# Attention values as the stationary operand, two outputs of a head side by side in TensorE's columns, turned back afterwards

## What is computed

```python
def attend(q, k, v, map_w):
    s = jnp.einsum('bqhmd,bkhmd->bhmqk', q, k).astype(jnp.float32)
    p = jax.nn.softmax(s, axis=-1)
    w = jnp.einsum('bhmqk,mh->bhqk', p, map_w.astype(jnp.float32))
    return jnp.einsum('bhqk,bkhd->bqhd', w.astype(v.dtype), v)
```

## Time and profile before

| what | value |
|---|---|
| profiled execution's own time | 4513.33 us |
| span of its instructions | 4511.4 us |
| mean granted TensorE clock | 0.92 |
| TensorE matmul busy | 3802.8 us (84%) |
| VectorE busy | 1758.7 us (39%) |
| ScalarE busy | 1679.3 us (37%) |
| L893, products with the values | 2624 records, 350.7 us busy |
| L882, transposes of probabilities | 1312 records, 225.2 us busy |
| L867, scores | 800 records |

### The profile page before, as it was taken

The page is one execution under the profiler, slowest core; times in us unless marked ns, Lnnn a source line. Parts: engine busy times, 40 slices in busy tenths (PEclk is TensorE's granted clock), DMA queues, the critical chain, the costliest instruction groups (busy, mean ns, idle before and its releaser), DMA issues. The chain is left out here.

```text
span 4511.4 us, 57439 instructions
## 1 busy us (share of the span) xinstructions
PE 3802.8 (84%) x20496; PEld 3071.4 (68%) x20496; DVE 1758.7 (39%) x2503; ACT 1679.3 (37%) x2683; POOL 326.6 (7%) x610
## 2 busy tenths in 40 slices
PE   4997677997987799999998699666998469999997
PEld 1997346776255687787797599444776348877875
DVE  2112754664323432233254411465665443322323
ACT  3113654664433322222243311655665532222222
POOL 0000062110000000000000000044110000000000
PEclk8998786999999899999999899878999689999998
DMA  4123220001732232232255222410000223322323
GB/s 161 58 84 121 95 64 6 7 5 74 292 118 101 84 98 85 87 98 86 86 171 178 102 85 72 154 54 29 7 5 26 70 93 98 94 87 89 94 93 126
DMA packets 128904, 398.45 MB, mean 88 GB/s; under 512 B 17392, under 2 KB 63664, under 8 KB 121136
## 3 DMA queue, kind: packets, MB, share of 16 engines
q1 hardware_dynamic: 105200, 327.21, 22.0%
q0 software_dynamic: 2880, 41.94, 2.3%
q10 hardware_dynamic: 20736, 28.18, 1.8%
HBM read 340.27 MB, written 57.02 MB: 88 GB/s over the span
## 5 line engine op out<-in xcount | busy, mean ns | idle before, releaser
L646 PE MATMUL psum<-part,part 128*128 128x512 f32 (+2 forms) x4240 | 1514.3, 357 | 228.8 <-DVE part L1459 227.8
L647 PE MATMUL psum<-part,part 128*128 128x512 f32 (+2 forms) x4240 | 1508.1, 356 | 0.0
L648 PE MATMUL psum<-part,part 128*128 128x512 f32 (+2 forms) x4240 | 1506.9, 355 | 0.0
L646 PEld LDWEIGHTS psum<-part,part 128*128 128x128 f32 x4240 | 806.9, 190 | 332.0 <-issue 237.0
L1459 DVE TENSOR_TENSOR part<-region,part 128x1024 fp32r<-128x1024 f32 (+4 forms) x446 | 550.5, 1236 | 1154.7 <-ACT part L1363 625.4
L647 PEld LDWEIGHTS psum<-part,part 128*128 128x128 f32 x4240 | 807.3, 190 | 93.7
L648 PEld LDWEIGHTS psum<-part,part 128*128 128x128 f32 x4240 | 806.2, 190 | 94.6
L1363 ACT CAST part<-region 128x1024 fp32r<-128x1024 f32 x220 | 230.6, 1048 | 561.0 <-PE psum L648 511.3
L1763 DVE TENSOR_REDUCE region<-psum 128x1 f32<-128x1280 f32 (+1 forms) x216 | 295.7, 1370 | 262.7 <-PE psum L867 262.4
L893 PE MATMUL psum<-region,region 128*128 128x64 f32 x2624 | 350.7, 273 | 4.2 <-ACT region L1281 4.2
L893 PEld LDWEIGHTS psum<-region,region 128*128 128x128 f32 x2624 | 330.5, 195 | 18.9 <-ACT region L1281 10.1
(11 more groups left out here) (207 smaller groups left out, 3191.0 us busy)
## 6 DMA issues: line engine op xcount, KB each, us to landing
region<-in_ffn_in SPq DMA_DIRECT2D x220, 512.0 KB, 3.5
region<-in_ffn_out SPq DMA_DIRECT2D x80, 704.0 KB, 4.0
region<-in_ada_w POOLq DMA_DIRECT2D x20, 2048.0 KB, 12.9
proj<-region ACTq DMA_DIRECT2D x16, 1720.0 KB, 11.2
region<-proj SPq DMA_DIRECT2D x20, 1376.0 KB, 5.7
region<-in_w_in SPq DMA_DIRECT2D x16, 1376.0 KB, 7.2
region<-proj SPq DMA_DIRECT2D x136, 128.0 KB, 2.3
region<-in_x SPq DMA_DIRECT2D x16, 640.0 KB, 8.0
```

The costliest lines, as they stand in the source:

```text
L646: mm(out, a[0], b[0], start=start, stop=False)
L647: mm(out, a[0], b[1], start=False, stop=False)
L648: return mm(out, a[1], b[0], start=False, stop=stop)
```

## The change

The operands of the product trade places. The values of one head and one output (128 keys x 64) are now the stationary operand, the turned probabilities (128 keys x 128 queries) move. The differential output (w = 1) goes to PSUM partitions 0 to 63, the latent one (w = 0) to partitions 64 to 127 of bank `VALUES`, one after the other for each key block. Both outputs of a head are therefore multiplied at the same time, and `A_PT` becomes two pairs of buffers. The sum comes out as 64 values x 128 queries for each output, so it has to be turned back: ScalarE copies it to `A_OT` (`keep_values`), TensorE transposes it (`turn_back`) into spare columns of the third bank of the scores that come next, and VectorE scales the two halves from there, after waiting for those scores.

`VALUE_LAG` becomes 10 half slots, and a head's products are four pieces of 3, 3, 2 and 2 key blocks of both outputs in six half slots (`PRODUCTS`): the first two pieces in slot 2, the other two in slot 0, none in slot 1. `keep_values` on ScalarE is in slot 1, before the two copies of turned pieces; `turn_back` on TensorE is in slot 0, before the scores; the scaling on VectorE is in slot 0, before `greatest`. The places of the turns do not change. After the last tile seven slots run without scores instead of three.

```diff
-        A_PT = [take(NT, P) for _ in range(2)]
+        A_PT = [[take(NT, P) for _ in range(2)], [region(R_QKD + (2 + j) * N, NT, P) for j in range(2)]]
+        A_OT = take(P)
...
-        TURN_LAG, VALUE_LAG = 5, 6
+        TURN_LAG, VALUE_LAG = 5, 10
+        KEEP_SLOTS, BACK_SLOTS = 7, 9
         PIECES = ((0, 4), (4, 8), (8, NT))
+        PRODUCTS = ((0, 3), (3, 6), (6, 8), (8, NT), None, None)
...
+                    def head(lag):
+                        if m % 3 != lag % 3:
+                            return None
+                        if m >= lag:
+                            return (i, (m - lag) // 3)
+                        return None if first else (i - 1, (m - lag) // 3 + NH)
...
-            for m in range(VALUE_LAG // 2):
+            for m in range(BACK_SLOTS - 2):
...
-                        sp.wait_ge(sem("att_kept"), a.outs(i, OUTS))
+                        sp.wait_ge(sem("att_kept"), a.heads(i, NH))
...
+                        if a.base and not begun(i) and m == 0:
+                            pe.wait_ge(sem("att_kept"), a.heads(0, 0))
+                        if backs:
+                            turn_back(m, *backs)
...
-                    def values(i, q, p):
-                        pe.wait_ge(sem("pt_kept"), a.step(i, q, p) + 1)
-                        if p == 0 and begun(a.outs(i, q)):
-                            pe.wait_ge(sem("att_kept"), a.outs(i, q))
-                        v = region(R_VD if q % 2 else R_VM, NT, 256)
-                        h = q // 2
-                        for kt in range(*a.pieces[p]):
-                            last = mm(bank(VALUES, HD), A_PT[q % 2][:, kt, :], v[:, kt, h * HD:(h + 1) * HD],
-                                      start=(kt == 0), stop=(kt == a.nk - 1))
-                        if p == a.per - 1:
+                    def values(i, h, p):
+                        first, end = a.products[p]
+                        piece = [j for j, x in enumerate(a.pieces) if x is not None and x[0] < end][-1]
+                        pe.wait_ge(sem("pt_kept"), a.step(i, 2 * h + 1, piece) + 1)
+                        if p == 0 and begun(a.heads(i, h)):
+                            pe.wait_ge(sem("ot_kept"), a.heads(i, h))
+                        for kt in range(first, end):
+                            for w, at in ((1, R_VD), (0, R_VM)):
+                                v = region(at, NT, 256)[:, kt, h * HD:(h + 1) * HD]
+                                last = mm(bank(VALUES, P)[(1 - w) * HD:(2 - w) * HD, :], v, A_PT[h % 2][w][:, kt, :],
+                                          start=(kt == 0), stop=(kt == a.nk - 1), skip_group_check=True)
+                        if a.last_product(p):
                             last.then_inc(sem("pv_made"), 1)
+                    def turn_back(m, i, h):
+                        pe.wait_ge(sem("ot_kept"), a.heads(i, h) + 1)
+                        at = (3 * (m % 2) + 2) * BANK + 2 * P
+                        nc.tensor.transpose(psum[:, at:at + P], A_OT, ident[:]).then_inc(sem("turned_back"), 1)
...
+                    def keep_values(i, h):
+                        act.wait_ge(sem("pv_made"), a.heads(i, h) + 1)
+                        if begun(a.heads(i, h)):
+                            act.wait_ge(sem("turned_back"), a.heads(i, h))
+                        nc.scalar.copy(A_OT, bank(VALUES, P)).then_inc(sem("ot_kept"), 1)
...
-                    def keep_values(i, q):
-                        h = q // 2
-                        rl, m = A_RL[:, q:q + 1], 3 * h + q % 2
-                        v.reciprocal(rl, A_L[:, m:m + 1])
+                    def keep_values(m, scores_of, i, h):
+                        v.reciprocal(A_RL[:, 2 * h:2 * h + 2], A_L[:, 3 * h:3 * h + 2])
                         dve.drain()
-                        dve.wait_ge(sem("pv_made"), a.outs(i, q) + 1)
-                        at = h * HD if q % 2 else (NH + h) * HD
-                        v.tensor_scalar(A_OUT[:, a.first + i, at:at + HD], bank(VALUES, HD), rl, None, ALU.mult
-                                        ).then_inc(sem("att_kept"), 1)
+                        if scores_of is not None:
+                            dve.wait_ge(sem("scored"), a.maps(scores_of, m) + 1)
+                        dve.wait_ge(sem("turned_back"), a.heads(i, h) + 1)
+                        back = (3 * (m % 2) + 2) * BANK + 2 * P
+                        for w in range(2):
+                            at = h * HD if w else (NH + h) * HD
+                            last = v.tensor_scalar(A_OUT[:, a.first + i, at:at + HD],
+                                                   psum[:, back + (1 - w) * HD:back + (2 - w) * HD],
+                                                   A_RL[:, 2 * h + w:2 * h + w + 1], None, ALU.mult)
+                        last.then_inc(sem("att_kept"), 1)
+                    def slot(m, i, joins, turns, products, keeps, backs):
+                        if backs:
+                            keep_values(m, i, *backs)
                         if i is not None:
                             greatest(m, i)
                         if joins:
                             join_maps(*joins)
```

More of the change, by code:

```diff
@@ L365, in att_pieces, with att_products @@
             return PIECES if nk == NT else ((0, CT), None, None)
+        def att_products(nk):
+            return PRODUCTS if nk == NT else ((0, CT), None, None, None, None, None)
         def att_tiles(count, eng, slot):
@@ L370, in tile, with half @@
                 for m in range(SLOTS):
-                    def before(lag, j):
+                    def half(lag, j, per):
                         at = 2 * m + j - lag
                         if at >= 0:
-                            return (i, at // 3, at % 3)
-                        return None if first else (i - 1, (at + HALVES) // 3, (at + HALVES) % 3)
+                            return (i, at // per, at % per)
+                        return None if first else (i - 1, (at + HALVES) // per, (at + HALVES) % per)
+                    def head(lag):
[4 more added lines that the diff above has]
+                        return None if first else (i - 1, (m - lag) // 3 + NH)
                     joins = None
@@ L378, in tile @@
                         joins = (i, m // 3 - 1) if m else (i - 1, NH - 1)
-                    slot(m, i, joins, [before(TURN_LAG, j) for j in range(2)], [before(VALUE_LAG, j) for j in range(2)])
+                    slot(m, i, joins, [half(TURN_LAG, j, 3) for j in range(2)], [half(VALUE_LAG, j, 6) for j in range(2)],
+                         head(KEEP_SLOTS), head(BACK_SLOTS))
             tile(0, True)
@@ L382, in att_tiles, with after, head_after @@
                 tile(i, False)
-            for m in range(VALUE_LAG // 2):
-                def after(lag, j):
+            for m in range(BACK_SLOTS - 2):
+                def after(lag, j, per):
                     at = 2 * m + j - lag + HALVES
-                    return (count - 1, at // 3, at % 3) if at < HALVES else None
-                slot(m, None, None if m else (count - 1, NH - 1), [after(TURN_LAG, j) for j in range(2)],
-                     [after(VALUE_LAG, j) for j in range(2)])
+                    return (count - 1, at // per, at % per) if at < HALVES else None
+                def head_after(lag):
+                    return (count - 1, (m - lag) // 3 + NH) if m % 3 == lag % 3 and m < lag else None
+                slot(m, None, None if m else (count - 1, NH - 1), [after(TURN_LAG, j, 3) for j in range(2)],
+                     [after(VALUE_LAG, j, 6) for j in range(2)], head_after(KEEP_SLOTS), head_after(BACK_SLOTS))
         class Att:
@@ L395, in __init__ @@
                 self.pieces = att_pieces(nk)
+                self.products = att_products(nk)
                 self.per = sum(p is not None for p in self.pieces)
@@ L403, in heads @@
                 return NH * (self.base + i) + h
-            def outs(self, i, q):
-                return OUTS * (self.base + i) + q
             def step(self, i, q, p):
@@ L412, in has, with multiplies, last_product @@
                 return at is not None and self.pieces[at[2]] is not None
+            def multiplies(self, at):
+                return at is not None and self.products[at[2]] is not None
+            def last_product(self, p):
+                return p + 1 == sum(x is not None for x in self.products)
         def att_loops(l):
@@ L851, in attend, with scores @@
                 for a in att_loops(l):
-                    def scores(m, i):
+                    def scores(m, i, backs):
                         h, r = m // 3, m % 3
@@ L898, in slot @@
-                    def slot(m, i, joins, turns, products):
+                    def values(i, h, p):
[10 more added lines that the diff above has]
+                        if a.last_product(p):
+                            last.then_inc(sem("pv_made"), 1)
@@ L899, in slot @@
+                    def turn_back(m, i, h):
```

(24 more changed lines are left out.)

## The result

The changed kernel takes 4657.8 us (median of 4 runs, 4647.71 to 4660.09) against 4516.12 us of the kernel before in the same comparison (4511.79 to 4518.31). The ratio is 1.0311, 95% interval 1.0293 to 1.0328: slower by 142 us. I had forecast slower, +79 us and at most 4650 us. The direction and the mechanism held; the size did not.

What follows compares the result with a forecast made beforehand. The prediction took a hand-over chain of 11.43 us a head, not TensorE's work, as the bound. It summed 4513.3 + 56 (chain) + 8 (ends) + 15 (clock) = 4592 us, median 4594, with 8-in-10 range 4550 to 4650.

Steps and rivals of the forecast that it cites:

- The bound: Attention loop: a chain of hand-overs between engines sums to the 11.43 us period; TensorE's 92% busy share is no proof.
- The halves side by side: New products: two 64-column halves run at a time, 12 records in 0.66 us, 8 records in 0.44 us.
- the rival on it: New products: halves with 64 columns each don't overlap, +0.86 us a head, 4647 us; chance 0.10.
- The mode changes: Between split and whole columns on TensorE: 0.12 us to enter, 0.16 to leave, 1.1 us a head.
- rows 4: Earlier profile rows of the scan: 32 records with 64 moving columns behind 32-column weights, each head in a column quarter.
- The chain: Steady attention loop: 0.50 + 0.40 = +0.90 us a head, bounds 0.52 and 1.40; +56 us over 62 periods.
- The term "0.50 us later": Slot 2: 12 product records and the turn back delay the fp32 scores by 0.50 us, bounds 0.22 and 0.80.
- The term of 0.40 for the scaling: Slot 0: VectorE's two scalings before the maxima add 0.40 us to the chain, bounds 0.30 and 0.60.
- The clock: Attention: the clock falls in a part of the heads, 15 falls or so, +15 us, bounds 0 and +64.
- The thin stretch: Around TensorE's wait for the join: matmuls in flight drop from 2.42 to some 1.5 to 1.9 of 3.4 us.
- The rival "falls in every head": Clock stays low in long stretches or falls in every head: another 40 to 60 us, 4645 us; chance 0.10.
- The ends: Layer ends +2.3 us each, eight context heads 0.4 us each; together +8 us, bounds 3 to 15.

Runs made afterwards that it cites:

- the kernel with both: Changed kernel with BACK_SLOTS 10 (turn back and scaling one slot later) and products moved off the way to the fp32 scores: 4481.05 us, ratio 0.9917.
- the experiment: For the scaling: VectorE's scaling moved after the maxima and join, on top of the changed kernel with the full idle product: 4545.51 us, ratio 1.0048.
- the idle product: Changed kernel plus a thrown-away product of 512 moving columns per head in TensorE's wait before the join's turn: 4579.38 us, ratio 1.0130.
- the small idle product: Changed kernel plus an idle product of 128 instead of 512 moving columns in the same wait: 4612.74 us, ratio 1.0198.

## Why the prediction came out as it did

**The bound: right.** The sum of 11.43 us around the loop, not the 92% of busy time, said what the loop could give back. At full clock a head gave back 0.6 us for the scaling, 0.7 for scaling and turn back, 1.0 for the burst of 12 with its changes, and 1.7 for all: the undisturbed period moved with what was taken off that chain.

**The halves side by side: right.** At full clock a burst of 12 records takes 0.88 us; less some 0.2 of pipeline that is the 0.66 us of six pairs. One by one at 0.11 they would need 1.3. Plainer still, bursts of 8, 12 and 16 records (the last in the kernel with both) take 0.66, 0.88 and 1.09 us, 0.055 us for each record more; the old bursts of 4 and 12 took 0.56 and 1.45, 0.11 us. Since the earlier trace rows only had quarters of the columns, this was the first row with halves, and the rival on it is out. The mode changes are as read from rows 4: the turn at 945.13 starts 0.08 before the burst's modelled end (945.21).

**The chain: right in sum, off in two terms that offset each other.** Forecast +0.90 us a head (0.52 to 1.40), measured +0.96 at full clock. The term "0.50 us later" for the scores in slot 2 came out as 1.56 - 0.83 = +0.73 less the 0.33 that the two steps before it became shorter, so +0.40. The term of 0.40 for the scaling was 0.57 in the timeline and 0.6 in the experiment. I had left out that the first scaling starts 0.2 us later behind the scores than the maxima had. So 0.10 us too much in one place and 0.17 too little in the other: that the sum came so close is partly luck.

**The clock: the step that failed.** I wrote "a part of the heads", "15 falls or so", "some 1 us late", +15 us. The thin stretch was read correctly, and its place too. But there were 47 falls, and three heads in four were hit. From the first to the last join of each layer there are 31 periods, 62 in all; their mean is 13.43 us, 11.37 before. Of these 2.06 us 0.96 are the chain; the other 1.10 x 62 = 68 us are the clock, above the upper bound of 64 that I gave the term. The experiment agrees: the idle product took 78 us out of the whole, some 6 of which are its shorter hand-over. Two things made my size wrong. The thin stretch comes back with every head, and I priced it as an occasional accident. And half of the falls lasted 6.8 us; a head with one of those is 2 us longer, where I had put 1, which is right for a fall of 3.4 us (13.4 us, or 13.2 to 13.4 with the small idle product). Why some last longer I take from the rows, no run tests it: in the first 3.4 us of the long fall at 952.60 TensorE still had gaps (2.79 us in flight), in the short one at 983.30 hardly any (3.38). The rival "falls in every head" had nearly the right price, 4645 us, and I gave it 0.10.

**The ends: 8 us forecast, some 19 measured.** The profiled executions differ by 4660.1 - 4513.3 = 147 us (the medians by 142), the 62 periods by 128. Last join to last scaling in layer 0 was 1099.4 to 1105.7 and is 1166.1 to 1176.4 us, +4.0 against the +2.3 forecast: the clock falls in that stretch too, and a burst of 24 records takes 2.65 us. In layer 1, at full clock, it takes 1.53, and the end is +2.4. The first latent scores start at 734.90 instead of 731.15, +3.8 against 3.2 for the context heads. The rest, some 9 us, I did not follow; from the last scaling of layer 0 to the first join of layer 1 it is 10 us more (2021.6 us before, 2031.9 now).

So 147 us = 60 (the chain, 0.96 x 62) + 68 (the clock) + 19 (the ends and what lies outside), where I had 56 + 15 + 8. What stays open is how much of the last kernel's gain is due to the new operands and how much to the new places of the steps: the old operands with such places were not tried.

## What to carry to other kernels

Sum the hand-overs around one turn of the loop and compare with its period, before an engine's busy share is taken for the bound; then a change is worth what it takes off that round, and each helper step (turn back, scaling) belongs where its engine waits. A speed-up beside the chain becomes idle time, and in a kernel near full TensorE load idle time may not be free: look for the thinnest stretch after the change, and if the clock can fall there, price one fall for each turn of the loop (here it fell in three turns of four, at 1 or 2 us each).

## What the runs showed of the hardware

- More work made the kernel faster: 0.86 us of thrown-away matmuls in each head took the time from 4657.8 to 4579.4 us, with the clock at 1.00 instead of 0.85, and 0.2 us of them gave rather more than half of that (4612.7 us).
- Two fp32 products with 64 weight columns each ran side by side: for the product line 156.1 us of busy time with 1194 records before, 86.1 us with 1200 in the last kernel, both at a clock of 0.99 or more:

```profile
L893 PE MATMUL psum<-region,region 128*128 128x64 f32 x1194 | 156.1, 269 | 0.0
```

```profile
L926 PE MATMUL psum<-region,region 128*64 128x128 f32 x1200 | 86.1, 282 | 0.0
```
